# A two-layer diffusion trunk on one core: Silu's table and the first accumulators ahead, and the last scatter between the last down products

## What is computed

```
x  = x + g1 * mixer(norm(x, mod))            # mod = silu(cond) @ mod_w[l] + mod_b[l]
h  = norm(x, mod)
a  = einsum('td,edf->etf', h, w_gate)        # 16 experts, 512 wide
b  = einsum('td,edf->etf', h, w_up)
hid = silu(a) * b * gates
x  = x + g2 * einsum('etf,efd->td', hid, w_down)
```

## Time and profile before

| | us |
|---|---|
| median of 3 runs | 860.23 |
| their range | 857.46 to 862.83 |
| the profiled execution's own time | 860.25 |
| its span, first to last instruction | 857.8 |

### The profile page before, as it was taken

The page is one execution under the profiler, slowest core; times in us unless marked ns, Lnnn a source line. Parts: engine busy times, 40 slices in busy tenths (PEclk is TensorE's granted clock), DMA queues, the critical chain, the costliest instruction groups (busy, mean ns, idle before and its releaser), DMA issues.

```text
span 857.8 us, 13351 instructions
## 1 busy us (share of the span) xinstructions
PE 818.7 (95%) x5760; PEld 511.7 (60%) x5760; DVE 284.1 (33%) x587; ACT 176.4 (21%) x308; POOL 38.0 (4%) x67
## 2 busy tenths in 40 slices
PE   4999999899999999999999999999899999999997
PEld 3777777787643555345436888788654554455534
DVE  2155533513731212111113844581542121121213
ACT  4056013511411101111013111300411111110111
POOL 4100000020200000000000000000120000000000
PEclk8999999999999999999999999999899999999999
DMA  9999866685699999999999969457489999999991
GB/s 342 370 316 368 303 231 236 238 308 200 219 390 424 420 425 424 421 426 424 427 415 386 381 213 334 148 180 310 162 332 422 424 424 421 424 422 425 425 418 61
DMA packets 69221, 292.54 MB, mean 341 GB/s; under 512 B 4017, under 2 KB 6182, under 8 KB 48628
## 3 DMA queue, kind: packets, MB, share of 16 engines
q1 hardware_dynamic: 67156, 289.70, 85.6%
q10 hardware_dynamic: 1248, 1.08, 0.5%
q0 software_dynamic: 768, 1.04, 0.4%
HBM read 290.10 MB, written 1.70 MB: 340 GB/s over the span
## 4 chain that ended last, share of the span: by engine, by line
PE 86%; DVE 8%; DMA 4%; ACT 1%; issue 1%; SPq 0%; DVEq 0%
PE ps L1955 25%; PE ps L1983 12%; PE ps L2093 6%; PE ps L1931 6%; PE ps L1535 5%; PE ps L1998 4%; PE ps L1599 4%; PE ps L1721 3%; PE ps L1807 3%; PE ps L1593 3%; PE ps L1574 3%; DMA ring<-in_moe_w_up 3%; PE ps L2089 1%; DVE xT L1205 1%; DVE hs L1175 1%
## 5 line engine op out<-in xcount | busy, mean ns | idle before, releaser
L1955 PE MATMUL ps<-ring,arena 128*64 128x512 f32 x832 | 223.6, 593 | 3.4 <-DMA ring<-in_moe_w_up 1.8
L1955 PEld LDWEIGHTS ps<-ring,arena 128*64 128x64 f32 x832 | 72.3, 137 | 111.1 <-issue 107.9
L1983 PE MATMUL ps<-ring,arena 128*64 128x512 f32 x512 | 113.4, 595 | 1.1 <-ACT arena L856 1.1
L1983 PEld LDWEIGHTS ps<-ring,arena 128*64 128x64 f32 x512 | 36.2, 137 | 66.4 <-issue 63.1
L1326 DVE SCALAR_TENSOR_TENSOR arena<-ps,arena 128x256 f32<-128x256 f32 x32 | 20.0, 666 | 153.1 <-PE ps L1955 153.1
L2093 PE MATMUL ps<-hs,ring 128*128 128x256 f32 x320 | 70.3, 380 | 0.0
L2093 PEld LDWEIGHTS ps<-hs,ring 128*128 128x128 f32 x320 | 60.5, 190 | 9.3 <-issue 1.4
L1931 PE MATMUL ps<-arena 128*128 (+1 forms) x512 | 60.0, 275 | 0.0
L1931 PEld LDWEIGHTS ps<-arena 128*128 128x128 f32 x512 | 58.4, 192 | 0.4 <-issue 0.4
L1955 PE MATMUL ps<-hs,arena 128*64 128x512 f32 x128 | 56.3, 593 | 0.0
L1535 PE MATMUL ps<-ring,csil 128*32 128x128 f32 x1536 | 50.9, 290 | 4.1 <-DVE arena L967 4.1
(11 more groups left out here) (312 smaller groups left out, 873.7 us busy)
## 6 DMA issues: line engine op xcount, KB each, us to landing
ring<-in_moe_w_up SPq DMA_DIRECT2D x64, 1024.0 KB, 15.8
ring<-in_moe_w_down SPq DMA_DIRECT2D x64, 1024.0 KB, 13.1
ring<-in_mod_w SPq DMA_DIRECT2D x24, 2048.0 KB, 12.9
ring<-in_moe_w_gate SPq DMA_DIRECT2D x20, 2048.0 KB, 13.2
hs<-in_moe_w_gate SPq DMA_DIRECT2D x8, 2048.0 KB, 15.2
ring<-in_hy_in_w SPq DMA_DIRECT2D x6, 2048.0 KB, 14.3
ring<-in_ab_in_w SPq DMA_DIRECT2D x4, 2048.0 KB, 12.7
arena<-in_moe_w_gate SPq DMA_DIRECT2D x4, 2048.0 KB, 15.0
```

The costliest lines, as they stand in the source:

```text
L1955: ins = mm(bank(4 + w)[e * 64:e * 64 + 64, :], xg[:, k, e * 64:e * 64 + 64], weights[:, k, :], start=(k == 0), stop=(k == KD - 1))
L1983: ins = mm(bank(6 + half)[e * 64:e * 64 + 64, :], hidT[:, f, e * 64:e * 64 + 64], down_unit(n + 4 + e)[:, f, half * 512:half * 512 + 512], ...
```

## The change

Three things in one. ScalarE, once two of POOL's constants are there, runs a Silu on one element per partition ahead of its first copy. TensorE opens the accumulators of banks 0 to 3 ahead of the sums of the squares, behind the same waits for xT (and one for POOL's constants), and no longer in the step "early". In each expert stage the last pair has its own routine, `last_down`: first output half complete, half of the second, scatter chunks 0 to 3, the rest of the second half, chunks 4 to 7; and VectorE does residual parts 0 and 1 ahead of its copy of the second half of y.

```diff
@@ ScalarE, ahead of the first copy
+            act.wait_ge(q["g_const"], 2)
+            act_fn(small[:, 92:93], eps[:], ACT.Silu)
             act.wait_ge(q["t_in"], 1)
             nc.scalar.copy(xf[:, 1024:2048], bank(2, 2)).then_inc(q["a_xT"], 1)
@@ VectorE, end of moe(l)
                 hidden(NPAIR - 1)
-                take_last()
                 if l == 0:
                     v.tensor_copy(hraw[:, :, NS * T:NS * T + NS], modT[:, 1, 0:8, :])
-                residual(l, 5, [0, 1, 2, 3])
+                residual(l, 5, [0, 1, 2, 3], parts=(0, 1))
+                take_last()
+                residual(l, 5, [0, 1, 2, 3], parts=(2, 3))
@@ TensorE, head
+            pe.wait_ge(q["g_const"], 8)
+            pe.wait_ge(q["a_xT"], 1)
+            pe.wait_ge(q["d_xT"], 1)
+            open_accumulators()
             norm(0)
...
                 elif what == "early":
-                    if a[0] == 0:
-                        pe.wait_ge(q["a_xT"], 1)
-                        pe.wait_ge(q["d_xT"], 1)
-                        open_accumulators()
@@ TensorE, moe(l)
+                def last_down():
+
+                    i = NPAIR - 1
+                    pe.wait_ge(q["a_hT"], i + (n0 + 1))
+                    pe.wait_ge(q["d_hT"], i + (n0 + 1))
+                    pe.wait_ge(q["down_low_in"], (i + (n0 + 1)) * 32)
+
+                    def rows_of_columns(half, fs):
+                        for f in fs:
+                            for e in range(2):
+                                ins = mm(bank(6 + half)[e * 64:e * 64 + 64, :], hidT[:, f, e * 64:e * 64 + 64],
+                                         down_unit(n + 4 + e)[:, f, half * 512:half * 512 + 512],
+                                         start=(f == 0), stop=(f == KF - 1))
+                                if half and f == KF - 1:
+                                    used(ins, n + 4 + e)
+                        return ins
+
+                    def scatter_chunks(ks):
+                        for k in ks:
+                            ins = mm(bank(0, 4)[:, k * 256:k * 256 + 256], y[:, k * 128:k * 128 + 128], ST7,
+                                     start=False, stop=False, skip_group_check=True)
+                            if k % 2:
+                                ins.then_inc(q["m_add"], 1)
+
+                    rows_of_columns(0, (0, 1))
+                    for e in range(2):
+                        arrived(pe, n + 4 + e, i)
+                    rows_of_columns(0, (2, 3)).then_inc(q["m_half"], 1)
+                    rows_of_columns(1, (0, 1)).then_inc(q["down_low_free"], 1)
+                    pe.wait_ge(q["a_y"], y0 + 4 * NPAIR - 3)
+                    scatter_chunks(range(0, 4))
+                    rows_of_columns(1, (2, 3))
+                    pe.wait_ge(q["d_y"], y0 + 4 * NPAIR - 3)
+                    scatter_chunks(range(4, KD))
...
-                down(NPAIR - 1, last=True)
-                last_scatter()
+                last_down()
```

More of the change, by code:

```diff
@@ L1538, in mod_row, with open_accumulators @@
                 used(ins, n)
+            def open_accumulators():
+                for b in range(4):
+                    mm(bank(b), zero16[:], zero16[:].rearrange("p (o c) -> p o c", o=1).broadcast_to([P, 4, 128]),
+                       start=True, stop=False, skip_group_check=True)
+            pe.wait_ge(q["g_const"], 8)
+            pe.wait_ge(q["a_xT"], 1)
+            pe.wait_ge(q["d_xT"], 1)
+            open_accumulators()
             norm(0)
@@ L1553, in h_ready @@
                 pe.wait_ge(q[sem_name], count)
[L1555 to L1559, removed]
             def h0_ready(k):
@@ L1969, in turn_hidden, with down @@
                     ins.then_inc(q["m_hT"], 1)
-                def down(i, last=False):
+                def last_down():
[28 more added lines that the diff above has]
+                    scatter_chunks(range(4, KD))
+                def down(i):
                     pe.wait_ge(q["a_hT"], i + (n0 + 1))
@@ L1987, in down @@
                                         used(ins, n + 4 + e)
-                            if last and 2 in fs and half == 0:
-                                ins.then_inc(q["m_half"], 1)
                         if 0 in fs:
@@ L2000, in scatter @@
                                skip_group_check=True)
[L2002 to L2011, removed]
                 pe.wait_ge(q["d_S"], 3 * l + 1)
```

## The result

The changed kernel takes 865.52 us (median of 8 runs, 864.03 to 870.57) beside 859.82 for the kernel before (8 runs, 857.46 to 862.83). The ratio of the runs is 1.0071 (the two medians alone make 1.0066), with a 95% interval of 1.0054 to 1.0087. A second set of 12 runs gave 863.23 (861.9 to 869.11), ratio 1.0047 [1.0028, 1.0065]. So the change costs some 4 to 6 us. The forecast was 0.7 us more (860.9), its range ended at 863.7; the time is within 1% of before, as forecast, but the slowing is real.

What follows compares the result with a forecast made beforehand. TensorE, busy 95% of the span, was taken to bound the kernel. From 860.25 us, less 1.0 at the kernel's start, plus 0.70 at the end of stage 0 and 0.95 at stage 1's, came 860.9 us; range 858.0 to 863.7.

Steps and rivals of the forecast that it cites:

- Silu's table: Kernel start, ScalarE: an early Silu removes one 1.28 us table load; at unchanged clock the norm row's copy comes 0.36 us earlier.
- The accumulators ahead: Kernel start, TensorE: moving the four opening matmuls is itself worth 0; the divided pause keeps the clock up.
- the 2.24 us at 13.58: TensorE's pause before the squares' sums; split into about 1.05 and 0.15 us, it would leave the clock at 2.4 GHz.
- The opening "from 12.4 to 13.4": Kernel start, TensorE: four matmuls, 1.04 us, fit before the sums at 13.58; at half speed 2.1 us, up to 0.6 lost.
- The uncovered copy: Expert stage ends: VectorE's copy delays chunk 4 to T + 9.83 (T: last down products' start), 0.95 us later; residual 0.70 later.
- The branch: End of stage 1, behind the scatter: the 0.51 us pause before the final transposes stays as it is, price 0.95 us.
- the second rival: Behind the scatter, the branch holds TensorE, counted from the copy's wait: stage 1 pays 1.86 us, total 861.8; chance 0.13.
- Weights and queues: Last down products: weights arrive with 2.0 us to spare; SP's load waits 2.8 us, costing nothing. Late-weights rival: 861.9, chance 0.04.
- The sum: Whole kernel: 860.25 - 1.0 + 0.70 + 0.95 = 860.9 us.
- tails: Ends of both expert stages, from the last down products on: 0.70 us lost in stage 0, 0.95 in stage 1, together 1.65.
- head: Kernel start up to the first input projections: 1.0 us gained, projections at about 23.5; bounds 1.0 gained, 0.6 lost.

Runs made afterwards that it cites:

- change, repeated: The changed kernel itself timed once more, against the kernel before: 863.23 us, ratio 1.0047.
- head alone: Kernel before with only Silu ahead and the accumulators' opening ahead, last scatter as before: 860.98 us, ratio 1.0015.
- accumulators alone: Kernel before with only the accumulators' opening moved ahead, ScalarE's order as before: 863.29 us, ratio 1.003.
- change, no branch: Changed kernel with TensorE's unused fallback and its branch left out behind both expert stages: 863.25 us, ratio 1.0019 against the kernel before.
- change, pause filled: Changed kernel with the opening issued three more times (12 matmuls with zeros) at its old place: 865.03 us, ratio 1.0047 against the kernel before.
- head, no branch: Kernel before with Silu and the accumulators' opening ahead, TensorE's fallback and branch left out behind both expert stages: 863.29 us, ratio 1.0032.
- both, no branch, filled: Changed kernel without TensorE's fallback and branch, the opening run three more times at its old place: 861.14 us, ratio 1.0005 against the kernel before.
- tails alone: Kernel before with only the last scatter's new order and the residual's new place, head as before: 863.92 us, ratio 1.0035.

## Why the prediction was wrong

**Silu's table.** Right in what happened (one load less, none at 14.4, copies and squares unharmed), and right that TensorE is late next. Worth nothing by itself: 1.0004.

**The accumulators ahead: the first failed step.** The prediction said that where they stood "they cost nothing", so the move is worth 0. They cost nothing there, but they did something: with them TensorE waited 0.75 us ahead of the first projections, without them 2.07 to 3.75 us. The prediction had used just such a pause, the 2.24 us at 13.58, as the reason for a low clock, and did not ask how long the pause is where the four matmuls leave; by its own figures (rows done at 21.1, projections at 23.5) it would be 2.4 us. The projections started at 25.14 in the change, not at 23.5. The modulation rows did get 1.6 us faster (3.70 for 5.30) in the change, but the projections wait for VectorE, whose chain started later there and not earlier (ScalarE's copy at 16.65, not 15.91); what the rows gained became pause. Where the clock falls in it or soon behind it, the projections take 15.7 to 16.7 us instead of 14.05. The stretch from x to the second projections shows the cases:

| kernel | opening us | pause us | projections us | stretch us |
|---|---|---|---|---|
| before | 1.04, old place | 0.75 | 14.05 | 36.15 |
| change | 1.87 | 3.74 | 16.67 | 39.39 |
| change, repeated | 1.87 | 3.75 | 14.05 | 36.77 |
| head alone | 1.86 | 2.07 | 14.05 | 36.77 |
| accumulators alone | 1.02 | 3.74 | 15.74 | 38.05 |
| change, no branch | 1.86 | 3.74 | 16.66 | 39.39 |
| change, pause filled | 1.86 | 1.04 | 14.05 | 36.81 |
| head, no branch | 1.02 | 3.20 | 14.05 | 35.62 |
| both, no branch, filled | 1.02 | 0.27 | 14.05 | 35.25 |

The Trainium skill, "TensorE: Matmul & The Clock Gate", section "What's actually happening", says that the number of matmuls that run at the low clock at a kernel's start varies from run to run of one kernel. The openings agree: the first rise of the clock that the trace records stands at 11.66 in the head without the branch, where the opening took 1.02 us, and at 21.32 in the head alone, where it took 1.86, and TensorE's work up to there is the same in both. Whether a pause lowers the clock varies too: the second and third lines are two executions of the same program.

**The opening "from 12.4 to 13.4".** Its start was right to half a microsecond (12.85); its length was right in some executions and 1.87 us in others, where it pushed the sums by 1.07 us. The prediction had this as its bound (2.1 us, a loss of up to 0.6) but took the full rate, since the last clock that it had seen recorded was no low one. The transposes' 3.34 us at 7.75, against 2.31 for the same 16 in the earlier trace rows, would have told that TensorE starts low.

**The uncovered copy.** The mechanism was right; the size was a little off. Chunk 4 started at 858.21 - 848.23 = T + 9.98 (forecast 9.83) and the residual ended at T + 13.31 in both stages (forecast 13.11): 0.90 us later than before in place of 0.70. Half a scatter takes 1.99 us in the timeline and not 1.86. Without the branch this is the whole price: 0.91 and 1.08 us.

**The branch: the second failed step, where the second rival was the right one.** The prediction kept the 0.51 us as a fixed pause, price 0.95 in stage 1. Counted from the end of the copy that TensorE waits for, the transposes start 3.43 us later before (851.12 - 847.69) and 3.81 us later in the change (861.96 - 857.46 - 0.69): they move with the wait, as the rival had it. The stage's price was 2.53 us against the rival's 1.86: the copy ended at T + 9.92 and not at T + 9.69 (0.23 us), and the hold was 0.38 us longer (3.81 for 3.43; its transfer of instructions took 1.25 us instead of 0.88). In the repetition the price was 2.18. The argument against it, that none shows in stage 0, was wrong too: stage 0 has one, 6.5 to 6.9 us after the wait. Before, 459.84 (the copy's end, 459.15 + 0.69) + 6.66 = 466.5, and the seventh sum came at 466.82 + 6 x 1.07/16 = 467.2: it was hidden by 0.7 us (an estimate from the tails alone; a transfer that ended at 464.89, and 1.54 to 1.60 us more, give 466.4 to 466.5), and the later wait brought it out. That costs another 1.0 us (1.95 less 0.91), in a place that the prediction costed at nothing.

**Weights and queues.** Right: no wait for weights inside the last down products in either stage. SP's load waits longer, as forecast (0.9 before; forecast 2.8), and nothing came of it:
```profile
SPq L466 <- PE ps L1985: 2.3, 1, 2.3
```

**The sum.** By the trace: tails 1.95 + 2.53 = 4.5 us in the first profile and 2.02 + 2.18 = 4.2 in the second, forecast 1.65; head +3.24 and +0.62, forecast -1.0. That is 7.7 and 4.8 us; the medians of the runs gave 5.7 (first set) and 3.5 (second). The parts measured apart, 1.0015 and 1.0035, make 1.0050, between the change's 1.0047 and 1.0071. Elsewhere the first profiled execution lost another 10.9 - 7.7 = 3.2 us against the profile of before, and the second gained 2.3 (its span is 2.5 us longer, with 4.8 by these parts). Much of that is the clock behind other pauses: 64 modulation products took 3.51 us in the first (at 235.42, behind a pause of 1.05 us), 1.95 in the second and 1.96 before; 64 others took 3.10 us before (at 139.67, soon behind a pause of 1.46 us) and 1.95 in the second (at 140.37). From the second projections to the last down products of stage 0, in a list of products that no kernel here alters, the 14 profiles take 404.7 to 410.4 us (before: 408.1). None of this is counted as part of the change's price. That the forecast had the sign right, 0.7 us slower, is partly luck: its head was a gain that did not come, and its tails were less than half of what they cost.

**What stays open.** Why one execution keeps the clock through 3.75 us of pause and another does not, and why the first rise of the clock comes early in some (10.92 to 12.63, opening 1.02 us) and late in others (16.63 to 21.32, opening 1.86 to 1.87 us). Whether it is the branch itself or the length of the fallback's code that makes TensorE wait for instructions: both went together, and no run kept the branch with a shorter fallback. What passes in the 1.5 us between the transfer's end and TensorE's next product. Why the no-branch kernel with both parts (1.0019) is not slower than its head alone (1.0032): the intervals overlap, since both spread over 9 us.

## What to carry to other kernels

An instruction that costs nothing where it stands may still be keeping an engine busy: before moving it, work out the pause that it leaves, not only the room that it finds. A pause with nothing to wait for in the timeline can be a wait for instructions: look at the transfers of the instruction queue, find the event from which it counts (here the last wait ahead of a branch), and ask of every edit that delays this event where the pause will come out, also some microseconds further on, where it is now hidden. Products added as filler move that place too. And splitting a sequence so that the consumer starts earlier pays only if the last piece's own chain (product, copy, scatter) keeps its cover.

## What the runs showed of the hardware

- TensorE stands still at a fixed place of its instruction list some time after the end of the copy that its last wait ahead of the branch names: 3.43 to 4.01 us in stage 1, right behind the branch, and 6.5 to 6.9 us in stage 0, 22 matmuls behind the scatter, 10 when 12 matmuls are added ahead and 8 when 14 are. It goes on 1.47 to 1.60 us after the end of a transfer of 16 384 bytes on the instruction queue, in all 14 places where this shows. Without the branch and its fallback neither pause shows, and the queue moves 35 or 36 such transfers instead of 39. The Trainium skill, "Runtime: NRT & Kernel Launch", section "Instruction fetch mechanics", says that instructions are fetched in blocks of a fixed size, in sequence, and that branching breaks this. The transfers of one size agree, and so does the pause that moves by as many matmuls as were added.
- After pauses of 3.74 and 3.75 us TensorE's granted clock went to 0.50 in one execution and stayed at 1.00 in another of the same program; the fall costs 1.7 to 2.6 us of the 14.05 us behind it.
- The granted clock reads 1.00 from the start although TensorE works at the low level: 16 transposes took 3.34 to 3.68 us at the start, 2.07 us behind products with zeros. The trace's first record is a rise to 1.00, at 10.60 us before and at 16.79 us in the change.
